# One core, two layers: TensorE's loops over the feed-forward blocks written out

## What is computed

```python
hn = rms_norm_2(h, norm_ffn[i])
h = h + jnp.square(jax.nn.relu(hn @ ffn_w1[i])) @ ffn_w2[i]      # 2048 -> 8192 -> 2048
gate = jax.nn.sigmoid(rms_norm_2(h, norm_ple[i]) @ ple_w_gate[i])  # 2048 -> 2048
h = h + (p[i] @ ple_w_proj[i]) * gate
return rms_norm_2(h, norm_final)
```

## Time and profile before

| | us |
|---|---|
| median of 3 runs | 2237.29 |
| lowest and highest | 2236.19, 2238.55 |
| the profiled execution | 2235.54 |
| its span in the trace | 2233.8 |
| TensorE's matmuls busy in the span | 2192.0 |
| TensorE's weight loads busy | 1898.2 |
| DVE, ACT busy | 1559.7, 1106.5 |

### The profile page before, as it was taken

The page is one execution under the profiler, slowest core; times in us unless marked ns, Lnnn a source line. Parts: engine busy times, 40 slices in busy tenths (PEclk is TensorE's granted clock), DMA queues, the critical chain, the costliest instruction groups (busy, mean ns, idle before and its releaser), DMA issues.

```text
span 2233.8 us, 41093 instructions
## 1 busy us (share of the span) xinstructions
PE 2192.0 (98%) x15436; PEld 1898.2 (85%) x15436; DVE 1559.7 (70%) x2393; ACT 1106.5 (50%) x1747; POOL 104.2 (5%) x94
## 2 busy tenths in 40 slices
PE   6999999999999999999999999999999999999997
PEld 5998888888888888888888878888888888888887
DVE  5975787887887577687666667665565575566767
ACT  2444545555554465465545545544444454445454
POOL 0000000000000010110000003000000000000202
PEclk7999999999999999999999999999999999999999
DMA  9995555445445577555544336555555555555552
GB/s 354 384 352 192 166 175 171 161 162 170 162 161 168 179 246 245 187 196 184 189 142 132 125 130 203 183 187 189 179 189 187 188 173 198 183 187 179 185 182 85
DMA packets 116082, 424.90 MB, mean 190 GB/s; under 512 B 13200, under 2 KB 13456, under 8 KB 115696
## 3 DMA queue, kind: packets, MB, share of 16 engines
q1 hardware_dynamic: 111744, 407.46, 54.0%
q0 software_dynamic: 4208, 15.60, 2.1%
HBM read 414.62 MB, written 8.39 MB: 189 GB/s over the span
## 4 chain that ended last, share of the span: by engine, by line
PE 93%; DVE 4%; ACT 2%; issue 1%; DMA 0%; SPq 0%; DVEq 0%; ACTq 0%
PE ps L2159 47%; PE ps L2160 23%; PE ps L2270 5%; PE ps L2539 3%; PE ps L2215 2%; PE ps L2216 2%; PE ps L2217 2%; PE ps L2540 1%; DVE wlo L1291 1%; PE ps L2692 1%; PE ps L2199 1%; ACT whi L716 1%; PE ps L2191 0%; DMA xt<-in_x 0%; DVE t L1508 0%
## 5 line engine op out<-in xcount | busy, mean ns | idle before, releaser
L2159 PE MATMUL ps<-acts,whi 128*128 128x512 f32 x3312 | 1202.6, 405 | 3.0 <-DVE wt L1297 1.3
L1291 DVE TENSOR_TENSOR wlo<-raw,whi 128x1024 fp32r<-128x1024 f32 x629 | 786.2, 1259 | 552.5 <-ACT whi L716 549.8
L716 ACT ACTIVATE whi<-raw 128x1024 fp32r<-128x1024 f32 x671 | 703.6, 1057 | 684.6 <-PE ps L2160 599.1
L2160 PE MATMUL ps<-acts,wlo 128*128 128x256 f32 x3312 | 926.6, 280 | 0.0
L2159 PEld LDWEIGHTS ps<-acts,whi 128*128 128x128 f32 x3312 | 621.5, 188 | 164.4 <-issue 8.7
L2160 PEld LDWEIGHTS ps<-acts,wlo 128*128 128x128 f32 x3312 | 625.1, 189 | 4.5 <-issue 3.4
L2159 PE MATMUL ps<-hidn,whi 128*128 128x512 f32 x1280 | 453.0, 398 | 2.2 <-DVE s L1297 1.7
L2160 PE MATMUL ps<-hidn,wlo 128*128 128x256 f32 x1280 | 357.7, 279 | 0.0
L2159 PEld LDWEIGHTS ps<-hidn,whi 128*128 128x128 f32 x1280 | 240.1, 188 | 64.9 <-DVE s L1297 4.3
L2160 PEld LDWEIGHTS ps<-hidn,wlo 128*128 128x128 f32 x1280 | 241.4, 189 | 0.5 <-issue 0.5
L716 ACT ACTIVATE half<-ps 128x256 f32<-128x256 f32 x333 | 125.0, 381 | 59.4 <-PE ps L2160 50.2
(11 more groups left out here) (337 smaller groups left out, 2039.8 us busy)
## 6 DMA issues: line engine op xcount, KB each, us to landing
raw<-in_stream SPq DMA_DIRECT2D x767, 512.0 KB, 4.0
gate_dram<-stage POOLq DMA_DIRECT2D x32, 128.0 KB, 2.6
gab<-gate_dram POOLq DMA_DIRECT2D x8, 512.0 KB, 6.6
xt<-in_x SPq DMA_DIRECT2D x1, 2048.0 KB, 9.7
xt<-in_x POOLq DMA_DIRECT2D x1, 2048.0 KB, 8.8
ple_dram<-pr__111 POOLq DMA_DIRECT2D x4, 512.0 KB, 3.7
pj<-ple_dram POOLq DMA_DIRECT2D x1, 2048.0 KB, 11.9
out<-y__143 SPq DMA_DIRECT2D x2, 512.0 KB, 2.8
```

The lines of the kernel that those rows point to most:

```text
L716: return nc.scalar.activation(dst, src, ACT.Copy)
L1291: tt(wlo[:, n % SPLIT, :], raw[:, in_stream(g) % RAW, :], whi[:, n % SPLIT, :].bitcast(F32), ALU.subtract).then_inc(raw_used, 1)
L2159: mm(ps[bank + n][:, :], whi[:, n0 % SPLIT, c:c + P], act[:, off + kt + k, :], start=kt + k == 0, stop=False)
L2160: ins = mm(ps[bank + n][:, 0:T], wlo[:, n0 % SPLIT, c:c + P], act[:, off + kt + k, 0:T], start=False, stop=kt + k == last)
```

## The change

Four loops in TensorE's program become Python loops, so that their bodies are written out one after the other, with b and f as constants. With that, each wait in them is for a constant where it was for a register's value. The work, its order and the programs of the other engines stay as they are.

```diff
             def ffn(f, first):
                 if first:
                     first_block(FF0, 2, 0, (E - 4, 0), sqb, 2, acts, 6, sqz, 20, 8)
-                with pe.Fori(1 if first else 0, 4) as b:
+                for b in range(1 if first else 0, 4):
                     block_of(FF0, f * 8 + b, acts, (f * 32 + b * 4, E - 4))
                 for j in range(8):
                     pe.wait_ge(s.relu_lo, f * 16 + (2 * j + 2))
                     use(FF0 + 32 + j, f * 8, RAW, hidn, 2 * j, evac=(f * 32, E + 12))
-                with pe.Fori(1, 4) as b:
+                for b in range(1, 4):
                     block_of(FF0 + 32, f * 8 + b, hidn, (f * 32 + b * 4, E + 12))
 
             ffn(0, True)
-            with pe.Fori(1, 4) as f:
+            for f in range(1, 4):
                 ffn(f, False)
             E += 128
 
             first_block(PG0, 3, 0, (E - 4, 0), sqb, 3, acts, 6, sqz, 24)
-            with pe.Fori(1, 3) as b:
+            for b in range(1, 3):
                 block_of(PG0, b, acts, (b * 4, E - 4))
```

## The result

The written-out loops made the kernel slower by about 5.5 us: the median is 2241.85 us (2238.94 to 2243.51, 14 runs) against 2236.31 us for the kernel before (2233.95 to 2238.71, 14 runs), a ratio of 1.0025 with an interval of 1.0018 to 1.0032. Later, beside other runs of before, it was 2241.43 against 2237.67 us, 1.002 [1.001, 1.003]. The profiled execution took 2240.44 us.

The account below looks back on a forecast made before the run. TensorE, busy 98% of the span, was taken as the bound; 2.0 us for paired waits plus 0.65 us for cadence, added to the 2237.29 us median, gave 2239.9 us, range 2236.0 to 2244.5.

Parts of the forecast that it names:

- the forecast case: Restarts in the feed-forward part and gate cost +2.0 us, with 12 to 22 long blocks: 2237.8 to 2241.5 us; chance 0.62.
- the cadence turns mostly long: Rival: the fixed restart distance makes 23 or more of 32 blocks long, 0.37 us each, up to 2245.2 us; chance 0.19.
- Step 1: TensorE's loop branches and register arithmetic at 32 restarts go; worth at most 1.6 us, taken as nothing because hidden.
- Step 2: Two constant waits on each block's first weight load delay it about 0.06 us at 32 restarts: +2.0 us.
- Step 3: Within blocks, matmuls keep a short or long rate set at the restart; +0.65 us taken, bounds -5.9 to +5.9.
- the 18 restarts in straight code: Restarts of the same matmuls in the old trace's straight code, 11 followed by the long rate; by them +1.3 us.
- Step 4: Written-out code sends some 26 more packets through TensorE's instruction queue; taken to cost nothing.
- Step 5: Waits of the other weight tiles, for wlo, accumulator banks and relu_lo, stay met long before; nothing.
- the five signs named: Expected afterwards: L1297 releases no restart loads, distance 0.11 to 0.12 us, 26 more packets, blocks 22.49 and 22.86 us.

Follow-up runs that it names:

- the clean pair of kernels with one cadence: Matmul order whi, wlo, wlo, whi in the changed kernel (2232.03 us, ratio 0.9991) and in the kernel before with its loops (2232.39 us, 0.9988).
- the second profile: The changed kernel run and profiled once more, unedited: 2241.43 us, ratio 1.002 to the kernel before.

## Why the prediction was right, and where it was wrong

The time fell in the range, 2 us above the number predicted, and just above the 2237.8 to 2241.5 us of the forecast case. That it stood so near is in part luck: the sum started from 2237.29 us, the median of three runs, and the 14 runs put the time before 1.0 us lower. Against these the change cost 5.5 us where 2.65 was the sum: slower, and by more than the 4.5 us that the prediction took for the least it could tell from no change. So the case that came is the rival "the cadence turns mostly long", which had 0.19, and not the forecast; the range holds it because it reached up to 2244.5 us for this rival.

**Step 1, branches and register arithmetic: right.** No load starts earlier behind the add than before. The 28 blocks without a restart wait take as long with loops as without (633.18 and 633.17 us), so the loops' bookkeeping was hidden even there. In the kernel before a branch that goes back takes 0.21 us, done before the restart.

**Step 2, the pair of waits: right, with its size.** The distance went from 0.052 to 0.115 us, the word from "DVE s L1297" to "issue", 32 more semaphore instructions stand in the trace, and the clean pair of kernels with one cadence gives 1.74 us over 27 restarts, 0.064 each, as priced. Exchanging the two waits took it away. Both numbers could be read from two restarts of the old trace.

**Step 3, the cadence: mechanism right in the main, size wrong.** What stands at the restart does change how many blocks are long: with the pair of waits 27 and 24 of 28, and 16 with the same code and the waits exchanged. The sum took 0.65 us for it; the 28 blocks show 27 long instead of 14, 13 x 0.36 = 4.7 us, and the second profile 24 instead of 14. The step that failed is the sample: I took the 18 restarts in straight code, 11 of them long, as draws from the same urn, and then halved their result towards the loops' share. They aren't draws of that kind. In the changed stretch a long block is followed by a long one nearly always. My reading is that each block hands its timing on: TensorE's last matmul starts ACT, ACT starts DVE, DVE starts TensorE, so a block that began in one way ends in the same way, and with one fixed distance everywhere the next begins like it. The straight restarts of before had the same distance of 0.115 us, but most stood singly, behind other work, and gave 11 long of 18. So the distance alone doesn't fix the rate; what went before counts too. My words in the rival, that a fixed distance may always land in the long rate, were the better reading, and six evacuations in a row in straight code, long each time, were nearer to this stretch than the 18 others. That long blocks follow long ones in this kernel is shown; that the chain over ACT and DVE does it is not. It speaks for it that the kernels with another distance (0.053, 0.13 to 0.20, 0.226 us) mix the rates again, and against it that a short block doesn't repeat: each of the five in the two profiles' 28 blocks is followed at once by a long one.

**Step 4, more code to fetch: right.** 26 packets more were predicted, and 94 became 120. They cost nothing in the 28 blocks: of three pairs of kernels, alike but for the loops, two agree to 0.01 us, and the third differs by just the pair of waits. The fetch does cost where it is a return to a large body, 0.6 us a turn; the change has no such loop.

**Step 5, the other waits: right.** No wait appeared within blocks: from 1355 to 2203 us both traces have the same 38 weight loads with more than 0.18 us of idle time ahead of them, all at restarts or in blocks that were straight before. The idle time of the whi loads in `down` rose from 49.5 to 51.4 us, of which the 15 changed restarts in `down` are 0.9 us. The rest is the ordinary spacing, which is wider in a long block.

**What would show it.** Four of the five signs named came: releaser, distance, packets, and short blocks of 22.49 and long ones of 22.86 (22.50 to 22.55 and 22.85 measured). The fifth, far more than half of the blocks long, was named as what would make the forecast wrong, and it did.

**Open.** What in TensorE makes two rates of one sequence of matmuls, 2.77 and 2.83 us a tile at a granted clock of 1.00, isn't settled. Turning the second pair's order leaves one rate of 2.787, so it has to do with how whi and wlo loads and matmuls follow each other; no run separated this further. In before's trace the whi loads of a long block follow each other by 345, 358 and 357 ns in turn, those of a short one by 345 to 350 ns. Nor is it known which distance gives which rate: with 0.115 us in a row of like blocks 51 of 56 were long, and 0.05, 0.13 to 0.20 and 0.23 us gave 30, 11 and 10 long ones (of 56, 28 and 28).

## What to carry to other kernels

Read the gap behind a restart to 0.01 us, with its releaser: where "issue" stands and no engine, look for a semaphore instruction of that engine just ahead. Of two waits on constants ahead of one instruction, write the one that comes late first; with waits on computed values it was the other way round here (0.05 us with the late one last, 0.13 to 0.20 with it first). Ahead of a change that moves timing by hundredths, look at the length of each block in order, not only at their mean: if blocks come in two lengths, the change may turn all of them to one, and that is worth more than the delay itself. Better still, remove both the wait, here by evacuating before the next tile is prepared, and the choice between two rates, here by the order of matmuls; the two together gave 11.5 to 15 us where the written-out loops lost 5.5.

## What the runs showed of the hardware

- The same matmuls ran at one of two steady rates, 2.773 or 2.827 us for eight pairs, at the same granted clock of 1.00, and with no waits between blocks the runs fell into two groups 13 us apart.
- The order whi, wlo, wlo, whi gave a single rate of 2.787 us for the eight pairs.
- One semaphore instruction (0.051 us in the trace) between the end of a wait and a load cost 0.063 us at the restart; the next one cost 0.11.
- Going back to the start of a loop with eight blocks of code took TensorE's branch 3.4 us each of two times, with the code fetched anew, and cost 0.6 us behind queued matmuls; in the loops of the kernel before, with one to three blocks of code, it took 0.21 us and cost nothing.
- The first 84 us of the program end up to 3.6 us apart between executions of the same instructions.
